# A hybrid attention layer: norm of the forgetting heads' output inside the attention stage, compression three couples later, and another order behind steps with extra work

## The chip, the cores and the metric

One core of one Trainium2 chip runs the whole layer in one launch. The metric is device time in microseconds (us), the median of several runs. The engines are TensorE (PE; PEld is its weight load), VectorE (DVE), ScalarE (ACT), GpSimd (POOL) and the DMA queue of SyncE (SP). Each runs its own instructions in order, and they meet at semaphores.

## The reference

The layer takes 512 prompt tokens and 8 sampled tokens (one each for 8 sequences with 256 cached positions), model width 1024, all in float32. Cut to what matters:

```python
hp  = half_ffn(x, ...)                               # x + 0.5 * rmsnorm(swiglu(rmsnorm(x)))
fq, fk, fv, logf, nq, nkv, ng = project(rmsnorm(hp), w_in, b_f, pos)
o_fox = fox_attention(fq, fk, fv, cumsum(logf), pos)     # 8 heads, forgetting bias, causal
o_nsa = nsa_attention(nq, ng, nkv, ...)                  # 8 heads: compressed + selected + window, gated
of = rmsnorm(o_fox.reshape(B, T, 512), g_fox)
on = rmsnorm(o_nsa.reshape(B, T, 512), g_nsa)
hp = hp + rmsnorm(concat([of, on]) @ w_out, g_mix_post)
y  = half_ffn(hp, ...)
# compress(x, w1, w2, pe): windows of 32 tokens, stride 16: gelu(hid) @ w2
```

The sampled tokens go through the same functions with the paged cache as keys and values. The two output norms (`of`, `on`) are separate, over 512 channels each.

## The kernel before

Activations lie transposed: 128 partitions of channels, 520 tokens along the free dimension. A weight item is 128 output channels; `products` multiplies it as a sum of three products of split halves (XH*WH, XL*WH, XH*WL), 8 channel tiles x 3 products x 2 token halves = 48 matmuls. ScalarE casts the high half of each item (L411), VectorE subtracts the low half (L414). The order is: first feed-forward, 23 items of the input projection, attention, 8 items of the output projection, second feed-forward.

**Attention** is 48 couples of (head, query tile) units, numbered m. Couples 0 to 15 are the forgetting heads, 16 to 47 the other heads' selected and window branches. The query tile is m mod 4, so scores are 128, 256, 384 and 512 columns wide in turn. The steps of the loop on TensorE are `scores(2m)` (L1559, the bias L1565, the mask L1567), the transposes of the weights of couple m-3 (`turn_p`, L1576), and the product with the values of couple m-4 (`weigh`, L1592). Scores of couple m need the exponentials of couple m-2, because four PSUM banks alternate. VectorE copies the even transposed unit out (L480), takes the maxima (`largest`, L1122), inverts the sums (L1128) and scales the weights of wide couples (L464); ScalarE copies the odd unit (L480), takes exponentials (L816) and copies finished output tiles to OT (`pair_out`, L800); GpSimd scales narrow couples (L464).

**Guests** are other work in PSUM banks 4 and 5 at fixed steps `AT_*`: first layer of the compression (AT_HIDDEN, step 11, L1622), its second layer (AT_CMP_KV, 15), compressed scores (AT_CMP_SCORES, 17, L1644), the decode's gate pick (AT_PICK, 18), its forgetting keys (AT_FOX_KEYS, 22, L1672), transposed compressed weights (AT_CMP_BACK, 25, L1652), the other decode keys (AT_NSA_KEYS, 26, L1681), transposed decode weights (AT_TURN, 30), decode values (AT_VALUES, 34, L1712) and the decode's output (AT_DECODED, 37). In a guest step TensorE first waits for the copies of the couple before (`banks_free`), runs the guest, `weigh(m-4)` and the scores of couple m+1, waits until the guest's banks are read (`emptied`), and only then does its `turn_p`. The functions `guest(m)` and `follow(m)` on the other engines hold the counterparts; on VectorE and ScalarE each step begins with the copy out (L480), then the maxima or exponentials.

SyncE loads what the guests need in one order: cache pages and shifted copies into X for the compression (L550 to L574), keys KF, KD and KW, values VS, then, after `cmp_back`, the forgetting values VF (L617), then VW (L621), and after `d_ot` (the decode's output) the output projection's weights.

**Behind attention**: ScalarE copies the last tile, both engines split the first two weight items, ScalarE squares 8 tiles of OT (L904), VectorE adds the squares (L1313), TensorE sums over partitions with a matrix of ones (L1441), ScalarE takes logarithm and exponential (L907, L910), VectorE multiplies (L1318), ScalarE and VectorE write the halves XH (L913) and XL (L944), while TensorE runs matmuls that nothing reads (L1448). Then 8 items are multiplied; VectorE copies each out of PSUM (L1327).

## Time and profile before

| | us |
|---|---|
| median of 3 runs | 1234.79 (1234.27 to 1239.14) |
| the profiled execution | 1235.9 |
| its span, first to last instruction | 1233.8 |
| PE busy | 1172.7 (95%) |
| DVE / ACT / POOL busy | 531.0 / 420.3 / 140.0 |
| mean granted TensorE clock | 0.977 of full speed |

Times in rows are counted from the start of the span. The granted clock is a share of 2.4 GHz, so 0.50 is the lower level of 1.2 GHz. Matmul ends are modelled, so starts are the safer numbers. An idle time stands in brackets with what ended it. Attention runs from 562 to 754 us, its end to the first product of the output projection from 754 to 770.

### The profile page before, as it was taken

How to read it: one execution, taken by the hardware profiler on the slowest of the kernel's cores; microseconds unless marked ns; L12 is line 12 of the kernel's file. 1: busy time of each engine (PE TensorE's matmuls, PEld its weight loads, DVE VectorE, ACT ScalarE, POOL GpSimd, SP SyncE). 2: the span in 40 equal slices, each digit the busy share in tenths (PEclk: the TensorE clock that was granted, in tenths of full speed). 3: DMA queues.
4: the chain of work that ended last, by engine and by line, in shares of the span. 5: the costliest groups of instructions: out<-in, count | busy, mean ns of one | idle time of the engine just before them, and what ended most of it. 6: DMA issues, size and time to landing. Idle time of an engine off the chain costs nothing.

```text
span 1233.8 us, 23263 instructions
## 1 busy us (share of the span) xinstructions
PE 1172.7 (95%) x9475; PEld 1078.7 (87%) x9482; DVE 531.0 (43%) x785; ACT 420.3 (34%) x731; POOL 140.0 (11%) x137
## 2 busy tenths in 40 slices
PE   8999999999999899998788997989999999999994
PEld 6999999999999799995354554979999999999994
DVE  3433433333333743454167676455343323333334
ACT  5322321222233642225144456444222221222332
POOL 0101100011111000222023110210011000011110
PEclk9999999999999999998889998999999999999997
DMA  7322223322223134216544311121222223232221
GB/s 273 103 71 99 86 78 110 104 74 96 78 86 112 54 121 139 85 61 157 119 121 120 121 69 35 69 69 43 95 102 78 70 101 112 85 103 87 67 86 70
DMA packets 49007, 117.52 MB, mean 95 GB/s; under 512 B 8186, under 2 KB 24954, under 8 KB 43138
## 3 DMA queue, kind: packets, MB, share of 16 engines
q1 hardware_dynamic: 45746, 110.55, 27.4%
q10 hardware_dynamic: 3184, 5.88, 1.3%
q8 instruction: 56, 0.92, 0.3%
q14 instruction: 21, 0.17, 0.0%
HBM read 107.79 MB, written 7.97 MB: 94 GB/s over the span
## 4 chain that ended last, share of the span: by engine, by line
PE 85%; DVE 6%; issue 3%; SPq 2%; ACT 2%; DMA 2%; DVEq 0%; ACTq 0%
PE ps L1432 75%; PE ps L1441 1%; PE ps L1622 1%; PE ps L1592 1%; PE ps L1559 1%; PE ps L1576 1%; DVE UT L964 1%; SPq L555 1%; DVE H L968 1%; DVE row_max L1122 1%; DVE PTS L480 1%; DVE XL L944 1%; DMA RAW<-in_w_gu 1%; DMA X<-X 1%; PE ps L1525 0%
## 5 line engine op out<-in xcount | busy, mean ns | idle before, releaser
L1432 PE MATMUL ps<-XH,WH 128*128 128x260 f32 x1904 | 389.8, 286 | 9.0 <-DVE XL L944 9.0
L1432 PE MATMUL ps<-XH,WL 128*128 128x260 f32 x1904 | 383.7, 283 | 0.0
L1432 PE MATMUL ps<-XL,WH 128*128 128x260 f32 x1904 | 383.2, 283 | 0.0
L411 ACT CAST WH<-RAW 128x1024 fp32r<-128x1024 f32 (+2 forms) x183 | 174.8, 956 | 528.1 <-PE ps L1432 525.9
L1432 PEld LDWEIGHTS ps<-XH,WH 128*128 128x128 f32 x1904 | 295.3, 189 | 14.9 <-DVE XL L944 10.3
L1432 PEld LDWEIGHTS ps<-XH,WL 128*128 128x128 f32 x1904 | 293.7, 189 | 0.0
L1432 PEld LDWEIGHTS ps<-XL,WH 128*128 128x128 f32 x1904 | 293.0, 188 | 0.0
L414 DVE TENSOR_TENSOR WL<-RAW,WH 128x1024 fp32r<-128x1024 f32 (+2 forms) x183 | 203.7, 1113 | 163.3 <-ACT WH L411 162.1
L1432 PE MATMUL ps<-UL,WH 128*128 128x260 f32 x704 | 141.9, 283 | 0.0
L1432 PE MATMUL ps<-UH,WL 128*128 128x260 f32 x704 | 141.5, 282 | 0.0
L1432 PE MATMUL ps<-UH,WH 128*128 128x260 f32 x704 | 141.3, 282 | 0.0
L1355 POOL TENSOR_TENSOR UL<-HT,UH 128x520 f32 (+1 forms) x44 | 57.8, 1315 | 634.8 <-ACT UH L692 634.8
L1432 PEld LDWEIGHTS ps<-UH,WL 128*128 128x128 f32 x704 | 108.5, 188 | 0.0
L1432 PEld LDWEIGHTS ps<-UH,WH 128*128 128x128 f32 x704 | 108.5, 188 | 0.0
L1432 PEld LDWEIGHTS ps<-UL,WH 128*128 128x128 f32 x704 | 108.4, 188 | 0.0
L984 DVE TENSOR_TENSOR UT<-ps,token_rstd 128x520 f32<-128x520 f32 x44 | 30.8, 700 | 145.8 <-PE ps L1432 145.8
L980 DVE TENSOR_TENSOR GT<-ps,token_rstd 128x520 f32<-128x520 f32 x44 | 30.8, 700 | 129.7 <-PE ps L1432 119.9
L692 ACT CAST UH<-HT 128x520 f32 (+1 forms) x44 | 27.6, 627 | 86.5 <-DVE HT L991 86.5
L1097 DVE TENSOR_TENSOR TR<-ps,token_rstd 128x520 f32<-128x520 f32 x23 | 16.1, 700 | 66.9 <-PE ps L1432 44.6
L1122 DVE TENSOR_REDUCE row_max<-ps 128x2 f32<-128x256 f32 (+3 forms) x48 | 39.1, 815 | 9.7 <-PE ps L1567 9.7
L816 ACT ACTIVATE PRB<-ps,row_max 128x384 f32<-128x384 f32 (+1 forms) x48 | 30.0, 630 | 25.6 <-DVE row_max L1122 24.5
L480 DVE COPY PTS<-ps 128x128 f32<-128x128 f32 (+3 forms) x48 | 23.5, 489 | 34.1 <-PE ps L1576 25.5
(239 smaller groups left out, 910.9 us busy)
## 6 DMA issues: line engine op xcount, KB each, us to landing
RAW<-in_w_gu SPq DMA_DIRECT2D x44, 1024.0 KB, 4.8
RAW<-in_w_down SPq DMA_DIRECT2D x16, 768.0 KB, 4.5
RAW<-in_w_in SPq DMA_DIRECT2D x11, 1024.0 KB, 5.0
RAW<-in_w_down SPq DMA_DIRECT2D x16, 640.0 KB, 4.3
KF<-in_fox_k SPq DMA_DIRECT2D x16, 256.0 KB, 4.2
VF<-in_fox_v SPq DMA_DIRECT2D x16, 256.0 KB, 5.0
RAW<-in_w_out SPq DMA_DIRECT2D x4, 1024.0 KB, 5.3
H<-in_x SPq DMA_DIRECT2D x4, 520.0 KB, 8.3
```

The lines of the kernel that those rows point to most:

```text
L411: nc.scalar.copy(WH[:, par, 0:width], RAW[:, slot, j, 0:width]).then_inc(w_hi, 1)
L414: nc.vector.tensor_tensor(WL[:, par, 0:width], RAW[:, slot, j, 0:width], WH[:, par, 0:width], ALU.subtract).then_inc(w_lo, 1)
L480: copy(PTS[:, w % PT_SLOTS, 0:i + 1, :], ps[:, 4 + w % 2, 0:P * (i + 1)].rearrange("p (a n) -> p a n", n=P)).then_inc(sem(name), 1)
L555: sp.dma_start(X[0:64, :, SEQ // PAGE + g, :, :].rearrange("p g n c -> p g (n c)"), I["nsa_t"][bass.ds(page[g], 1), :, 0:2, :].rearrange(" ...
L692: nc.scalar.copy(row(UH, st.m), HT[:, st.par, :]).then_inc(sem("hid_hi"), 1)
L816: nc.scalar.activation(weights(v)[:, 0:W], ps[:, score_bank(v), 0:W], ACT.Exp, bias=row_max[:, v:v + 1], accum_out=row_sum[:, v:v + 1]).th ...
L980: nc.vector.tensor_tensor(two(GT[:, st.par, :]), halves(0), two(R1[:, :]), ALU.mult).then_inc(sem("evac"), 1)
L984: nc.vector.tensor_tensor(two(UT[:, st.par, :]), halves(1), two(R1[:, :]), ALU.mult).then_inc(sem("evac"), 1)
L1097: nc.vector.tensor_tensor(two(TR[:, j % 4, :]), halves(j % 2), two(R1[:, :]), ALU.mult).then_inc(sem("projected"), 1)
L1122: nc.vector.reduce_max(row_max[:, v:v + 2], ps[:, score_bank(v):score_bank(v) + 2, 0:W], AX.X, negate=True).then_inc(sem("att_max"), 1)
L1355: nc.gpsimd.tensor_tensor(row(UL, st.m), HT[:, st.par, :], row(UH, st.m), ALU.subtract).then_inc(sem("hid_lo"), 1)
L1432: q = nc.tensor.matmul(ps[:, 2 * slot + half, 0:HALF], w[:, par, cols], x[:, kt0 + kt, half * HALF:(half + 1) * HALF], start=first and kt ...
```

## The change

1. The guest steps move: AT_HIDDEN 11 to 14, AT_CMP_KV 15 to 18, AT_CMP_SCORES 17 to 20, AT_CMP_BACK 25 to 27, AT_PICK 18 to 19, AT_NSA_KEYS 26 to 25, AT_TURN 30 to 29, AT_VALUES 34 to 32, AT_DECODED 37 to 35; AT_FOX_KEYS stays at 22. A guest AT_SUMS is added at 40.
2. In a step behind a guest VectorE takes the maxima and ScalarE the exponentials before the copy out.
3. The decode queries are filled in by 6 wider copies instead of 16, and the 8 copies of the new keys into KF go from VectorE to GpSimd, at step 17.
4. Eight of the sixteen loads of VF are issued ahead of the wait for `cmp_back`.
5. The forgetting heads' norm is computed in steps 36 to 48: squares on ScalarE, their sums on GpSimd, the partition sum on TensorE at 40, logarithm and exponential on ScalarE, the multiplication on GpSimd, XH on ScalarE and XL on VectorE. The first two weight items are split in steps 41 to 43. OSQ moves to another region.
6. Behind attention only tiles 4 to 7 are left. TensorE multiplies the ready tiles 0 to 3 of items 0 and 1 around the second partition sum; the matmuls that nothing reads are gone there.

```diff
-AT_HIDDEN, AT_CMP_KV, AT_CMP_SCORES, AT_CMP_BACK = 11, 15, 17, 25
-AT_PICK, AT_FOX_KEYS, AT_NSA_KEYS, AT_TURN, AT_VALUES, AT_DECODED = 18, 22, 26, 30, 34, 37
+AT_HIDDEN, AT_CMP_KV, AT_CMP_SCORES, AT_CMP_BACK = 14, 18, 20, 27
+AT_PICK, AT_FOX_KEYS, AT_NSA_KEYS, AT_TURN, AT_VALUES, AT_DECODED, AT_SUMS = 19, 22, 25, 29, 32, 35, 40
...
-            sp.wait_ge(sem("cmp_back"), 2)
-            for g in range(NPAGE):
+            for g in (*range(8, NPAGE), *range(8)):
+                if g == 0:
+                    sp.wait_ge(sem("cmp_back"), 2)
                 sp.dma_start(VF[g // 8][:, g % 8, :],
@@ ScalarE @@
+                elif m == AT_SUMS:
+                    output_log(0)
...
+                elif m == AT_DECODED + 1:
+                    act.wait_ge(sem("o_all"), 1)
+                    act.wait_ge(sem("att_out"), 5)
+                    output_square(0)
+                    output_square(1)
+                elif m == AT_DECODED + 2:
+                    output_square(2)
+                    output_square(3)
+                elif m == AT_DECODED + 3:
+                    output_square(4)
+                elif m == AT_SUMS:
+                    output_rstd(0)
+                    act.wait_ge(sem("att_out"), 6)
+                    act.wait_ge(sem("oacc"), 3)
+                    output_square(5)
+                elif m in (AT_SUMS + 1, AT_SUMS + 2):
+                    split(IT_OUT + m - AT_SUMS - 1)
+                elif AT_SUMS + 4 <= m < AT_SUMS + 8:
+                    output_high(m - AT_SUMS - 4)
+                elif m == AT_SUMS + 8:
+                    act.wait_ge(sem("att_out"), 7)
+                    output_square(6)
...
+                    if m < PAIRS and m - 1 in GUESTS:
+                        exponentials(m)
                     if m >= 3 and m not in GUESTS:
                         turn_out(act, nc.scalar.copy, 2 * (m - 3) + 1, "att_odd_out")
-                    if m < PAIRS:
+                    if m < PAIRS and m - 1 not in GUESTS:
                         exponentials(m)
...
+            output_square(7)
+            output_log(1)
+            output_rstd(1)
+            for t in range(4, 8):
+                output_high(t)
@@ VectorE @@
-                    for h in range(HF):
-                        nc.vector.tensor_copy(view(QBF[part, h // 2, :], h, [[128, 2], [40, 4]]), ...)
-                        q = nc.vector.tensor_copy(view(QBN[kv, :], h, [[128, 2], [40, 4]]), ...)
+                    for odd in (0, 1):
+                        part = slice(64 * odd, 64 * odd + 64)
+                        nc.vector.tensor_copy(view(QBF[part, :, :], odd, [[DEC * 32 + 2, 4], [128, 2], [40, 4]]), ...)
+                        for kv in range(HKV):
+                            q = nc.vector.tensor_copy(
+                                view(QBN[64 * kv:64 * kv + 64, :], 4 * kv + odd, [[2, 2], [128, 2], [40, 4]]), ...)
                     q.then_inc(sem("qb_filled"), 1)
-                    for n in range(DEC):
-                        q = nc.vector.tensor_copy(KF[n][:, :, PAST], fk_new[:, :, KF_ORDER[n]])
-                    q.then_inc(sem("kf_new"), 1)
...
+                if m in (AT_SUMS + 2, AT_SUMS + 3):
+                    split(IT_OUT + m - AT_SUMS - 2)
+                if AT_SUMS + 5 <= m < AT_SUMS + 9:
+                    low("o", "out", m - AT_SUMS - 5)
...
+                    if m < PAIRS and m - 1 in GUESTS:
+                        largest(m)
                     if m >= 3 and m not in GUESTS:
                         turn_out(dve, nc.vector.tensor_copy, 2 * (m - 3), "att_even_out")
-                    if m < PAIRS:
+                    if m < PAIRS and m - 1 not in GUESTS:
                         largest(m)
@@ GpSimd @@
+                if m == AT_PICK - 2:
+                    pool.wait_ge(sem("att_scored"), 4 * HF)
+                    nc.gpsimd.memset(QBF[:, :, :], 0.0).then_inc(sem("qb_cleared"), 1)
+                    pool.wait_ge(sem("cmp_hid"), 2)
+                    for n in range(DEC):
+                        q = nc.gpsimd.tensor_copy(KF[n][:, :, PAST], fk_new[:, :, KF_ORDER[n]])
+                    q.then_inc(sem("kf_new"), 1)
...
-                elif m == AT_CMP_SCORES + 8:
+                elif m == AT_FOX_KEYS + 1:
...
+                elif m == AT_DECODED + 2:
+                    output_sum(1)
+                    output_sum(2)
+                    output_sum(3)
+                elif m == AT_SUMS:
+                    output_sum(5)
+                elif AT_SUMS + 1 <= m < AT_SUMS + 5:
+                    t = m - AT_SUMS - 1
+                    pool.wait_ge(sem("orstd"), 1)
+                    nc.gpsimd.tensor_tensor(OT[:, t, :], OT[:, t, :], OR[:, 0, :], ALU.mult).then_inc(
+                        sem("onormed"), 1)
...
             attention()
+            output_sum(6)
@@ TensorE @@
+                elif m == AT_SUMS:
+                    pe.wait_ge(sem("oacc"), 3)
+                    all_partitions(OACC[:, 0, :], 2).then_inc(sem("oss"), 1)
...
+                elif m == AT_SUMS:
+                    pe.wait_ge(sem("oss_ln"), 1)
...
-            for g in (0, 1):
-                pe.wait_ge(sem("oacc"), 3 * g + 3)
-                all_partitions(OACC[:, g, :], 2 + g).then_inc(sem("oss"), 1)
-            keep_warm(WARM[2], bank=0)
+            def operand(t, kt):
+                if t == 0:
+                    pe.wait_ge(sem("xlo"), since("xlo", "o", kt + 1))
+                cols = slice(kt * P, kt * P + P)
+                for p, (w, x) in enumerate(((WH, XH), (WH, XL), (WL, XH))):
+                    for half in (0, 1):
+                        q = nc.tensor.matmul(ps[:, 2 * t + half, 0:HALF], w[:, (IT_OUT + t) % 2, cols], ...)
+                return q
...
+            ready(IT_OUT)
+            operand(0, 0)
+            operand(0, 1)
+            pe.wait_ge(sem("oacc"), 5)
+            all_partitions(OACC[:, 1, :], 2, stop=False)
+            pe.wait_ge(sem("osq"), 8)
+            all_partitions(OSQ[:, 2, :], 2, start=False).then_inc(sem("oss"), 1)
+            operand(0, 2)
+            operand(0, 3)
+            ready(IT_OUT + 1)
+            for kt in range(4):
+                operand(1, kt)
+            for t, kt in ((0, 4), (0, 5), (1, 4), (0, 6)):
+                operand(t, kt)
+            operand(0, 7).then_inc(used, 1)
+            operand(1, 5)
+            operand(1, 6)
+            operand(1, 7).then_inc(used, 1)
+            for t in range(2, KT):
```

## Rows read from the trace of the kernel before

**Rows 1.** Windows by stage: engines' busy time, granted clock, DMA share, GB/s.
```profile
722.00:754.00 32.00, 29.99 (x278) 19.07 (x275) 21.11 (x47) 17.83 (x55) 5.06 (x10) 1.00 0.16 64
754.00:769.90 15.90, 9.03 (x28) 4.72 (x29) 10.70 (x15) 11.67 (x19) 0.00 (x0) 0.68 0.21 66
```

**Rows 2.** Timeline of TensorE around the first layer of the compression.
```profile
580.25 0.39 PE L1576 MATMUL ps<-consts,PRA 128*128 128x128 f32 x2
...
587.13 1.04 PE L1576 MATMUL ps<-consts,PRB 128*128 128x128 f32 x8
...
597.20 18.38 PE L1622 MATMUL ps<-X,W 128*128 128x336 f32 x32 [6.51 <-DMA X<-X]
```

**Rows 3.** Timeline of TensorE in step 21.
```profile
656.11 0.85 PE L1576 MATMUL ps<-consts,PRB 128*128 128x128 f32 x6 [2.08 <-DVE PTS L480]
```

**Rows 4.** Timeline of VectorE in step 19: 16 copies like the first, then KF.
```profile
652.54 0.16 DVE L1237 COPY QBN<-nq_new 64x8 f32<-64x8 f32 x1
...
654.97 0.67 DVE L1241 COPY KF<-fk_new 128x4 f32<-128x4 f32 x8
```

**Rows 5.** Windows (columns as in group 1): the clock behind the compressed scores and behind step 21.
```profile
638.00:647.00 9.00, 8.38 (x50) 5.44 (x48) 3.99 (x7) 1.71 (x5) 2.09 (x3) 0.50 0.00 0
656.50:661.00 4.50, 4.15 (x35) 1.77 (x36) 4.43 (x9) 2.25 (x9) 0.61 (x2) 0.63 0.65 170
```

**Rows 6.** Timeline of TensorE: the same product at either clock.
```profile
638.43 1.12 PE L1592 MATMUL ps<-PTS,VTF 128*64 128x128 f32 x8
...
656.89 0.66 PE L1592 MATMUL ps<-PTS,VTN 128*64 128x128 f32 x8
```

**Rows 7.** Timeline of TensorE: waits of and behind guests.
```profile
671.55 1.06 PE L1652 MATMUL ps<-consts,SCM 128*128 128x128 f32 x8
...
674.74 0.87 PE L1576 MATMUL ps<-consts,PRB 128*128 128x128 f32 x6 [0.47 <-ACT PCT L841]
...
676.29 1.93 PE L1681 MATMUL ps<-KD,QBN 128*32 128x257 f32 x16 [0.68 <-ACT PTS L480]
...
718.85 0.70 PE L1559 MATMUL ps<-KXN,QXN 64*128 64x256 f32 x4 [1.07 <-ACT PRB L816]
```

**Rows 8.** Timeline of ScalarE: the idle time ahead of a wide couple's exponentials.
```profile
736.81 0.69 ACT L816 ACTIVATE PRB<-ps,row_max 128x512 f32<-128x512 f32 x1 [1.08 <-DVE row_max L1122]
```

**Rows 9.** Timeline of ScalarE behind attention.
```profile
754.07 0.59 ACT L800 COPY OT<-ps 128x512 f32<-128x512 f32 x1 [2.39 <-PE ps L1599]
...
756.45 0.64 ACT L904 ACTIVATE OACC<-OT 128x520 f32<-128x520 f32 x1
...
764.89 0.69 ACT L907 ACTIVATE OR<-ps,consts 128x520 f32<-128x520 f32 x1 [1.05 <-PE ps L1441]
765.61 0.64 ACT L910 ACTIVATE OR<-OR 128x520 f32<-128x520 f32 x1
...
774.79 0.73 ACT L913 ACTIVATE XH<-OT,gains 128x520 fp32r<-128x520 f32 x1 [0.55 <-DVE OT L1318]
```

**Rows 10.** Timeline of VectorE behind attention.
```profile
774.07 0.69 DVE L1318 TENSOR_TENSOR OT<-OT,OR 128x520 f32<-128x520 f32 x1
774.68 0.75 DVE L944 SCALAR_TENSOR_TENSOR XL<-OT,gains,XH 128x520 fp32r<-128x520 f32 x1
...
778.61 1.23 DVE L414 TENSOR_TENSOR WL<-RAW,WH 128x1024 fp32r<-128x1024 f32 x1 [0.45 <-ACT WH L411]
783.18 0.70 DVE L1327 COPY Y<-ps 128x520 f32<-128x520 f32 x1 [3.34 <-PE ps L1432]
```

**Rows 11.** The chain of waits: one item, and a partition sum at full clock.
```profile
507.02 5.72 PE ps L1432 x48
...
835.92 0.88 PE ps L1441 x4
```

**Rows 12.** GpSimd: 18 additions of squares, and one beside VectorE's subtraction.
```profile
L1348 POOL TENSOR_TENSOR ACC<-ACC,SQ x18: 1303/1315/1886, 358.3 to 1210.4; 128x520 f32<-128x520 f32 x18
...
784.85 1.87 POOL L1348 TENSOR_TENSOR ACC<-ACC,SQ 128x520 f32<-128x520 f32 x1 [4.54 <-ACT SQ L640]
```

More of the change, by code:

```diff
@@ L67 @@
 GUESTS = (AT_HIDDEN, AT_CMP_KV, AT_CMP_SCORES, AT_CMP_BACK, AT_PICK, AT_FOX_KEYS, AT_NSA_KEYS, AT_TURN, AT_VALUES,
-          AT_DECODED)
+          AT_DECODED, AT_SUMS)
 TILES = (["fg"] + ["fq"] * 4 + ["fk"] * 4 + ["fv"] * 4
@@ L822, in decode_exp, with output_square, output_log, output_rstd @@
                                      accum_out=dsum[:, n:n + 1]).then_inc(sem("d_exp"), 1)
+            def output_square(t):
+                dst = OACC[:, t // 4, :] if t % 4 == 0 else OSQ[:, t % 4 - 1, :]
+                nc.scalar.activation(dst, OT[:, t, :], ACT.Square).then_inc(sem("osq"), 1)
+            def output_log(g):
+                act.wait_ge(sem("oss"), g + 1)
+                nc.scalar.activation(two(OR[:, g, :]), halves(2), ACT.Ln, scale=1.0 / 512,
+                                     bias=const("eps")[:, 0:1]).then_inc(sem("oss_ln"), 1)
+            def output_rstd(g):
+                act.wait_ge(sem("oss_ln"), g + 1)
+                nc.scalar.activation(OR[:, g, :], OR[:, g, :], ACT.Exp, scale=-0.5).then_inc(sem("orstd"), 1)
+            def output_high(t):
+                act.wait_ge(sem("onormed"), t + 1)
+                nc.scalar.activation(XH[:, t, :], OT[:, t, :], ACT.Copy, scale=gain("out", t)).then_inc(
+                    sem("xhi"), 1)
             def guest(m):
@@ L1280, in follow @@
                                             ALU.mult).then_inc(sem("d_pn"), 1)
-                elif m == AT_VALUES:
+                if m == AT_VALUES:
                     nc.vector.reduce_sum(OS[:, 0, :], view(EF[:, :, :, :], 0, [[1, DH], [DH, 2 * HF]]), AX.X)
@@ L1818, in _ @@
             attention()
-            for g in (0, 1):
-                pe.wait_ge(sem("oacc"), 3 * g + 3)
-                all_partitions(OACC[:, g, :], 2 + g).then_inc(sem("oss"), 1)
-            keep_warm(WARM[2], bank=0)
-            for t in range(KT):
+            def operand(t, kt):
[4 more added lines that the diff above has]
+                    for half in (0, 1):
+                        q = nc.tensor.matmul(ps[:, 2 * t + half, 0:HALF], w[:, (IT_OUT + t) % 2, cols],
+                                             x[:, kt, half * HALF:(half + 1) * HALF],
+                                             start=kt == 0 and p == 0, stop=kt == KT - 1 and p == 2)
+                return q
[18 more added lines that the diff above has]
+            for t in range(2, KT):
                 ready(IT_OUT + t)
```

85 lines of the change are left out of this document (30 added, 55 removed).

## The prediction

> **What bounds the kernel now.** I read the page first: TensorE is busy for 1172.7 of 1233.8 us, so time is won where it stands idle or runs at 1.2 GHz. The windows by stage say where the change touches such time: between 722 and 754 us TensorE works 29.99 of 32 us at granted clock 1.00, and between 754 and 770 only 9.03 of 15.9 at 0.68, of which most is matmuls that nothing reads [rows 1]. The timeline of TensorE then shows single waits: 6.51 us for the shifted copies of X at step 11 [rows 2], 2.08 us for VectorE's copy out [rows 3], and waits of 0.4 to 1.1 us around guests [rows 7]. In the windows the reader is to see the clock: 0.50 for 9 us behind the 64 tiny matmuls of the compressed scores, and 0.63 behind the wait of rows 3 [rows 5]. What one such us costs is in rows 6: the same eight matmuls take 1.12 us at 0.50 and 0.66 at 1.00.
>
> **The change part by part.**
>
> *Compression at step 14.* Ahead of the guest there now stand the transposes and products of steps 11 to 13 and the scores of 12 to 14. The same pieces one cycle of four couples earlier run from 580.25 to the transposes at 587.13: 6.9 us [rows 2]. TensorE was free from about 590.7 (597.20 less 6.51), so it comes to the guest at 597.6, and the copies of X, which depend on nothing that moved, release it at 597.2. The work fills the wait: -6.5. If the copies came later, the difference would be waited for, so the gain lies between 0 (copies 6.5 late) and 6.5; they are queued behind nothing new, so I take -6.5.
>
> *Queries and keys of the decode.* In step 19 VectorE made 16 copies and eight into KF, from 652.5 to 655.6, 3.1 us, ahead of a copy out that TensorE stood still for, 2.08 us [rows 3, 4]. Now 6 copies remain, some 1.1 us by the spacing in rows 4, and the KF copies are on GpSimd three steps early. They stand in step 20 behind the 1.2 us maximum of the compressed scores, ahead of the maxima of 21 and the copy out that the forgetting keys at 22 wait for (`banks_free`), so some wait returns there: I take 0.5. With it goes the dip to 0.63 over 4.5 us, in which TensorE was busy for 4.15 [rows 5]: 0.37 of that is 1.5, but much of it is in small matmuls that such a dip need not stretch, so I take -0.6, and part of the waits next to it, -0.5. Sum -2.1 - 0.6 - 0.5 + 0.5 = -2.7; bounds -4 and 0. The 9 us at 0.50 behind the compressed scores stay: the 64 matmuls are unchanged and now have the tiny pick next to them. GpSimd's eight tiny copies have no row; between 0.1 us (VectorE's, rows 4) and 1.3 us (a full one, rows 12) each they take 1 to 10 us. They run in steps 17 to 19; steps 18 and 19 are scaled by VectorE, so even the long end only delays the scaling of couple 20, needed at 23. I cost it at nothing.
>
> *Maxima and exponentials first.* Behind a guest the scores are ready before the transposes. The 1.07 us behind AT_VALUES is of that kind [rows 7]; there are eleven guests, so I take that and half as much again for the others. Against it, the copy out comes up to 1.2 us later. -1.5; bounds -3 and +1.
>
> *AT_CMP_BACK at 27.* `weigh(23)` in that same step needs both copies of the transposed weights. Before, the guest came two steps ahead, and `emptied` cost 0.47 [rows 7]. Now ScalarE's copy of 0.6 us stands behind the exponentials of a wide couple: from the end of its scores 1.2 (maxima) + 1.35 + 0.6 = 3.3 us with the hand-overs, while TensorE has 1.06 (guest) and 1.09 (`weigh`). Wait 1.2 to 1.4, less 0.47: +0.9; bounds 0 and 1.5. Of the SyncE queue: eight VF loads go earlier; eight and VW still follow `cmp_back`, with about 15 us until AT_VALUES at 32. I cost that at nothing.
>
> *AT_SUMS.* One partition sum, 0.88 us [rows 11], and one more `banks_free`, 0.68 as in rows 7, taken as 0.5: +1.4. The wait for `oss_ln` lies beside `weigh(36)` and the scores of 41, 1.3 us, against 0.7 of the logarithm.
>
> *Work on the other engines, steps 36 to 48.* ScalarE gets 7 squares, a logarithm, an exponential, four XH at 0.64 to 0.73 us and two splits at 1.05: 4.5 + 1.3 + 2.9 + 2.1 = 10.8 us [rows 9]; it has 32 - 17.8 = 14.2 free [rows 1]. VectorE gets 2 x 1.23 + 4 x 0.75 = 5.5 [rows 10], with 10.9 free. Before a wide couple's exponentials ScalarE is idle for 1.08 us [rows 8], which hides a square or an XH. What shows: VectorE's split in step 43, whose idle time is smaller, +0.5, and the last couple, where nothing runs ahead: `low` twice (1.5 us, partly in its waits) ahead of the last copies out, +1.3. Sum +1.8; bounds 0 and, if all of ScalarE's work is on the path, +10.8.
>
> *Behind attention.* Let E be the end of the last product, 754.0 [rows 9]. Before, item 2 starts when item 1 is done, at 783.18 [rows 10], E + 29.2. Now: copy 0.6 and square 0.64, E + 1.2. TensorE meanwhile does tiles 0 and 1 of item 0, 12 of an item's 48 matmuls, 1.44 us [rows 11]. The two partition sums take 1.8: E + 3.2. Logarithm and exponential 1.4, multiplication 0.69, XH 0.73, XL 0.75 [rows 9, 10]: XL of tile 4 at E + 6.9, tile 5, 6 and 7 at 1.3 us intervals (VectorE's 0.69 + 0.75, overlapped by 0.1), the last at E + 10.8. TensorE's six ready pieces of 0.72 fill E + 3.2 to E + 7.5; tiles 4, 5, 4, 6 run to E + 10.4; tile 7 ends at E + 11.6, and the last three of item 1 at E + 13.8. Item 2's WL comes 2.4 us after item 0 (783.18 less 5.7 to 778.61 + 1.23), E + 14.0; I take E + 14.1. 29.2 - 14.1 = 15.1: -15.1. Below that TensorE can't go by more than its waits, 13.3 us of work, -15.9; if the clock fell to 0.68 as before [rows 1], the 13.3 us would take 6.3 more.
>
> Sum: -6.5 - 2.7 - 1.5 + 0.9 + 1.4 + 1.8 - 15.1 = -21.7. From the profiled execution's 1235.9 that is 1214.2. The median shown is 1234.8, 1.1 lower, so 1213.1.
>
> **A rule weighed.** GpSimd's additions of squares take 1.315 us alone and 1.87 where they start inside VectorE's two-input subtraction [rows 12]: one of the two waits. The Trainium skill, SBUF — State Buffer, "Who interferes with whom", says that the two engines share one pair of ports, that the instruction that starts first holds it for its whole length, and that VectorE's two-input operations and its two-port `tensor_scalar` both need it. By that rule, the trace agrees for GpSimd as the one who waits; the other order is no row here.
>
> **The rivals.**
> 1. *ScalarE or VectorE bounds steps 36 to 48.* For it: 10.8 us into 14.2 free, in an order of instructions that leaves no choice; ScalarE's free time comes in pieces of 0.4 to 1.1 us. Against it: TensorE is the one that is full (94%). If most of ScalarE's work is on the path, 8.5 instead of 1.8: 1220.
> 2. *GpSimd holds up VectorE.* Four sums and four multiplications of 1.3 us run beside VectorE's scaling. If each delays one scaling by half its length and half of that is hidden, 8 x 0.65 / 2 = 2.6: 1215.7. This is the rule above as a mechanism.
> 3. *The clock falls behind attention.* The last step's waits are longer than before and the sums come early; at 0.68 the gain there is 8.8 instead of 15.1: 1219.4.
> 4. *Slower: the attention stage stays at 1.2 GHz.* Guests 18, 19 and 20 now stand together, with tiny matmuls in each, at the place where the clock was 0.50 for 9 us [rows 5]. A step of some 2.4 us takes 1.7 times as long there [rows 6], 1.7 us more. If 15 more steps ran so, +25: 1238. It decides from 13 such steps on. Against it: before, the clock came back in four steps.
> 5. *The moved guests don't do what they say*, because X or VF comes later than TensorE: the 6.5 and the 2.7 go, 1222.
>
> **Chances.** Forecast 0.58, rival 1 0.18, rival 2 0.10, rival 3 0.06, rival 4 0.03, rival 5 0.05. The range starts at 1205, with every bound of the middle terms low (-1.3, -1.5, -0.9, -1.8 and some waits that I have not seen), and ends at 1222, with rivals 1, 2, 3 and 5 in it. A change of 0.5%, 6.2 us, is about what a measurement of this kernel can tell. Only rival 4 is outside on the other side: faster 0.95, same 0.02, slower 0.03.
>
> **What would show it.** Right: in the profile after, the first layer of the compression starts at 597 to 598 with a wait under 0.5 us; no wait for the copy out of 2 us behind it; the window from the last product of attention to item 2 is 14 us at clock 1.00; a wait of 1 to 1.5 us in step 27. Wrong: steps 36 to 48 longer than 34 us with waits for ScalarE's exponentials (rival 1); GpSimd's additions or VectorE's scalings longer than alone (rival 2); a clock under 0.9 behind attention (rival 3); a stretch of 0.50 longer than 12 us (rival 4). A time above 1222 would mean that a wait at the decode's guests that I cost at nothing is there.

## The result, and the profile after

| | before | after |
|---|---|---|
| median | 1234.68 (1233.69 to 1239.14, 7 runs) | 1228.88 (1225.81 to 1230.65, 7 runs) |
| the profiled execution | 1235.9 | 1230.65 |
| its span | 1233.8 | 1228.8 |
| DVE / ACT / POOL busy | 531.0 / 420.3 / 140.0 | 528.4 / 419.2 / 153.8 |

The ratio of after to before is 0.995, interval 0.9935 to 0.9965: 5.8 us faster, where 21.7 were forecast and 1205 was the low end and 1222 the high end of the range. The time lies 6.9 us above that range.

A stretch is told here from the start of `scores(m)` (the first matmul of couple m's scores) to that of another, since these exist in every kernel. "Lead" is how much earlier after reaches a point than before.

| us from the span's start | before | after | lead |
|---|---|---|---|
| scores of 28 | 686.26 | 682.21 | 4.1 |
| scores of 36 | 716.26 | 714.42 | 1.8 |
| scores of 40 | 727.08 | 724.26 | 2.8 |
| scores of 47 | 743.74 | 750.33 | -6.6 |
| last product of attention ends | 753.97 | 763.98 | -10.0 |
| item 2 starts | 783.2 | 778.01 | 5.2 |

So attention ends 10.0 us later instead of 6.6 earlier (21.7 less 15.1), and the stretch behind it does what was forecast: 29.2 us before, 14.0 now. The windows of after (columns as in rows 1) show the two stages of [rows 1] again:

```profile
722.00:754.00 32.00, 26.64 (x206) 15.86 (x204) 24.43 (x43) 20.38 (x58) 17.05 (x18) 0.89 0.11 34
764.00:778.00 14.00, 13.53 (x104) 12.88 (x104) 7.41 (x11) 7.81 (x12) 0.82 (x1) 1.00 0.00 1
```

The reader is to see the fifth engine: GpSimd's busy time in the same 32 us went from 5.06 to 17.05, TensorE's went from 29.99 to 26.64 and the granted clock from 1.00 to 0.89. Behind attention TensorE is busy 13.53 of 14 us at 1.00.

**GpSimd's queue.** ScalarE's last two squares, then GpSimd's timeline in after, steps 37 to 47:

```profile
720.28 1.16 ACT L827 ACTIVATE OSQ<-OT 128x520 f32<-128x520 f32 x2
```

```profile
722.33 1.09 POOL L464 TENSOR_SCALAR PRA<-PRA,row_inv,gates 128x256 f32<-128x256 f32 x2 [1.95 <-DVE row_inv L1159]
723.38 4.14 POOL L1445 TENSOR_TENSOR OACC<-OACC,OSQ 128x520 f32<-128x520 f32 x3
...
737.12 1.98 POOL L464 TENSOR_SCALAR PRA<-PRA,row_inv,gates 128x256 f32<-128x256 f32 x2 [1.28 <-DVE row_inv L1159]
739.07 4.00 POOL L1436 TENSOR_TENSOR OT<-OT,OR 128x520 f32<-128x520 f32 x3
...
756.23 1.28 POOL L1445 TENSOR_TENSOR OACC<-OACC,OSQ 128x520 f32<-128x520 f32 x1 [3.79 <-ACT OSQ L827]
```

The squares are all there at 721.4, but the three additions stand in the queue behind the scaling of a narrow couple that is ready only at 722.3, and run together from 723.4. VectorE beside them (timeline of VectorE, its scalings L464 and the subtractions L414 and L975):

```profile
724.76 2.97 DVE L464 TENSOR_SCALAR PRB<-PRB,row_inv,gates 128x384 f32<-128x384 f32 x2
...
736.94 1.20 DVE L414 TENSOR_TENSOR WL<-RAW,WH 128x1024 fp32r<-128x1024 f32 x1
739.58 2.35 DVE L464 TENSOR_SCALAR PRB<-PRB,row_inv,gates 128x384 f32<-128x384 f32 x2
741.86 2.30 DVE L414 TENSOR_TENSOR WL<-RAW,WH 128x1024 fp32r<-128x1024 f32 x1
...
753.36 0.87 DVE L464 TENSOR_SCALAR PRB<-PRB,row_inv,gates 128x384 f32<-128x384 f32 x2
...
756.26 1.81 DVE L975 SCALAR_TENSOR_TENSOR XL<-OT,gains,XH 128x520 fp32r<-128x520 f32 x1
```

The same pair of scalings takes 0.87 at 753.36, with GpSimd idle, and 2.97 and 2.35 where an addition or a multiplication of GpSimd is under way; the weight's subtraction 1.20 and 2.30; XL 0.75 [rows 10] and 1.81. TensorE is what waits for these (its timeline, steps 40 to 48):

```profile
727.66 1.99 PE L1492 MATMUL ps<-OACC,consts 128*128 128x260 f32 x4 [2.69 <-POOL OACC L1445]
...
744.63 1.36 PE L1627 MATMUL ps<-consts,PRB 128*128 128x128 f32 x6 [2.15 <-DVE PTS L480]
755.38 0.90 PE L1627 MATMUL ps<-consts,PRB 128*128 128x128 f32 x6 [1.50 <-DVE PTS L480]
758.68 1.94 PE L1627 MATMUL ps<-consts,PRB 128*128 128x128 f32 x8 [1.82 <-DVE PTS L480]
```

These are four waits, 8.2 us in all, and behind the first, the second and the last the clock falls. Windows of after:

```profile
728.00:730.00 2.00, 2.00 (x8) 1.02 (x7) 1.14 (x4) 1.11 (x5) 0.00 (x0) 0.50 0.00 0
744.00:748.00 4.00, 3.37 (x18) 2.22 (x18) 3.69 (x10) 3.15 (x12) 0.83 (x1) 0.60 0.68 202
758.00:764.00 6.00, 5.32 (x40) 4.37 (x41) 1.23 (x3) 0.58 (x1) 0.00 (x0) 0.72 0.00 0
```

The partition sum shows it in one row: 1.99 us at 0.50, against 0.88 at full clock [rows 11].

**The guests.** TensorE's waits of after at them, to be held against [rows 2, 3, 7]:

```profile
596.96 18.28 PE L1673 MATMUL ps<-X,W 128*128 128x336 f32 x32 [2.05 <-DMA X<-X]
...
629.41 0.87 PE L1682 MATMUL ps<-HID,W 128*128 128x160 f32 x2 [2.37 <-DVE HID L1250]
...
666.43 1.93 PE L1732 MATMUL ps<-KD,QBN 128*32 128x257 f32 x8 [2.27 <-DVE KW L1287]
...
681.15 1.12 PE L1650 MATMUL ps<-PCT,VCZ 128*128 128x512 f32 x2 [1.05 <-ACT PCT L860]
```

The 2.08 us of [rows 3] is gone and the 6.51 of [rows 2] became 2.05. The wait at the compression's second layer (2.37) was 1.80 in before, and a new one of 2.27 stands at the other decode keys, which moved from step 26 to 25. VectorE's timeline ahead of it:

```profile
661.84 1.21 DVE L1273 TENSOR_REDUCE csum<-SCM 128x32 f32<-128x1024 f32 x1
663.08 0.35 DVE L1274 RECIPROCAL csum<-csum 128x32 f32<-128x32 f32 x1
...
664.44 1.00 DVE L464 TENSOR_SCALAR PRB<-PRB,row_inv,gates 128x512 f32<-128x512 f32 x2
665.36 0.15 DVE L1281 RECIPROCAL dinv<-dsum 64x1 f32<-64x1 f32 x1
665.54 0.35 DVE L1282 TENSOR_SCALAR SF<-SF,dinv 64x257 f32<-64x257 f32 x1
665.92 0.17 DVE L1285 COPY KD<-nk_new 128x8 f32<-128x8 f32 x1
666.01 0.17 DVE L1287 COPY KW<-nk_new 128x8 f32<-128x8 f32 x1
```

VectorE works without a gap, and two copies of 0.17 us that depend on none of it stand last. The clock falls here too, in the window behind the wait:

```profile
666.00:670.00 4.00, 3.57 (x31) 1.90 (x32) 0.83 (x4) 1.02 (x4) 2.99 (x4) 0.57 0.00 0
```

### The profile page after: what moved, and what is told of

The parts are those of the page before. It is cut to its first block, busy times and chain, and to the rows that moved or that the text cites. A ratio compares the mean times of both kernels' runs of the same rounds, so it can differ in the third digit from the quotient of the medians.

```text
span 1228.8 us, 23220 instructions
## 1 busy us (share of the span) xinstructions
PE 1169.5 (95%) x9460; PEld 1080.0 (88%) x9466; DVE 528.4 (43%) x757; ACT 419.2 (34%) x731; POOL 153.8 (13%) x154
## 4 chain that ended last, share of the span: by engine, by line
PE 86%; DVE 6%; issue 2%; SPq 2%; ACT 2%; DMA 1%; POOL 0%; DVEq 0%; ACTq 0%; POOLq 0%
PE ps L1483 75%; PE ps L1492 2%; PE ps L1673 1%; PE ps L1643 1%; PE ps L1610 1%; PE ps L1627 1%; DVE UT L995 1%; SPq L555 1%; DVE H L999 1%; DVE row_max L1153 1%; DVE PTS L480 1%; DMA X<-X 1%; PE ps L1884 1%; DVE XL L975 1%; PE ps L1576 0%
## 5 line engine op out<-in xcount | busy, mean ns | idle before, releaser
L1483 PE MATMUL ps<-XH,WH 128*128 128x260 f32 x1872 | 383.4, 286 | 8.4 <-DVE XL L975 8.0
L1483 PE MATMUL ps<-XH,WL 128*128 128x260 f32 x1872 | 377.6, 283 | 0.0
L1483 PE MATMUL ps<-XL,WH 128*128 128x260 f32 x1872 | 377.0, 283 | 0.0
L1483 PEld LDWEIGHTS ps<-XH,WH 128*128 128x128 f32 x1872 | 290.7, 189 | 13.1 <-DVE XL L975 8.3
L1483 PEld LDWEIGHTS ps<-XH,WL 128*128 128x128 f32 x1872 | 289.0, 189 | 0.0
L1483 PEld LDWEIGHTS ps<-XL,WH 128*128 128x128 f32 x1872 | 288.3, 189 | 0.0
L414 DVE TENSOR_TENSOR WL<-RAW,WH 128x1024 fp32r<-128x1024 f32 (+2 forms) x183 | 204.8, 1119 | 158.1 <-ACT WH L411 156.8
L1483 PEld LDWEIGHTS ps<-UL,WH 128*128 128x128 f32 x704 | 108.3, 188 | 0.0
L1373 POOL TENSOR_TENSOR ACC<-ACC,SQ 128x520 f32<-128x520 f32 x18 | 27.0, 1499 | 93.1 <-ACT SQ L641 93.1
```

Of the source, the lines that this page charges most:

```text
L414: nc.vector.tensor_tensor(WL[:, par, 0:width], RAW[:, slot, j, 0:width], WH[:, par, 0:width], ALU.subtract).then_inc(w_lo, 1)
L1373: nc.gpsimd.tensor_tensor(ACC[:, :], ACC[:, :], SQ[:, par, :], ALU.add).then_inc(sem("acc"), 1)
L1483: q = nc.tensor.matmul(ps[:, 2 * slot + half, 0:HALF], w[:, par, cols], x[:, kt0 + kt, half * HALF:(half + 1) * HALF], start=first and kt ...
```

## The experiments

Twelve kernels ran in three groups, each group beside runs of the kernel before. Single executions of one kernel spread over 1 to 9 us (before: 1229.4 to 1238.6 in 23 runs), so differences of under 2 us between two experiments are read from stretches of the trace and not from medians.

| kernel | median | ratio to before, 95% | scores of 40 to end of attention |
|---|---|---|---|
| after | 1228.88 | 0.9950, 0.9935 to 0.9965 | 39.7 |
| norm off | 1230.75 | 0.9982, 0.9964 to 1.0000 | 26.9 |
| order back | 1227.91 | 0.9960, 0.9943 to 0.9978 | 40.7 |
| sums on TensorE | 1227.45 | 0.9965, 0.9943 to 0.9987 | 36.3 |
| fills for the norm | 1223.70 | 0.9929, 0.9905 to 0.9953 | 33.0 |
| guests back | 1233.53 | 1.0009, 0.9990 to 1.0027 | 26.9 |
| late guests back | 1229.91 | 0.9970, 0.9955 to 0.9985 | 26.9 |
| keys on GpSimd | 1227.93 | 0.9951, 0.9934 to 0.9969 | 26.9 |
| multiplications on VectorE | 1223.85 | 0.9926, 0.9900 to 0.9952 | 35.3 |
| reductions later | 1226.85 | 0.9942, 0.9924 to 0.9960 | 26.9 |
| lows late | 1221.72 | 0.9899, 0.9882 to 0.9915 | 31.8 |
| all edits | 1217.80 | 0.9873, 0.9856 to 0.9889 | 31.8 |
| all edits, old order | 1216.09 | 0.9853, 0.9830 to 0.9876 | 31.8 |

Before has 26.9 in the last column. The medians of before were 1233.6 (norm off to fills), 1233.0 (guests back to multiplications) and 1233.7 (the last four).

**Norm off.** Parts 5 and 6 of the change undone, parts 1 to 4 kept.

```diff
-                elif m == AT_DECODED + 2:
-                    output_sum(1)
...
-                elif AT_SUMS + 1 <= m < AT_SUMS + 5:
...
+            for g in (0, 1):
+                pe.wait_ge(sem("oacc"), 3 * g + 3)
```

> The changed kernel without parts 5 and 6 (the norm is computed behind attention as before, all other parts kept). The table of score starts shows the changed kernel 1.5 to 2.8 us ahead at steps 36 to 40 and 10.0 us behind at the end of attention. Theory A (the norm's own work in steps 36 to 48 is what costs the 12.8 us): the 15.1 us behind attention are lost again and about 12.8 are won back, 1228.9 + 2.3 = 1231, and the last product of attention ends 2 to 4 us earlier than in the kernel before, at 750 to 752. Rival B (the moved guests and the new order upset the late steps as well): attention ends at 755 or later and the time is 1236 or more.

Its trace takes 26.9 us from the scores of 40 to the end, as before, and its lead of 3.1 us stays constant there. So all 12.8 us that attention lost behind step 40 come from parts 5 and 6, and at the end of attention the guests, copies and order together give 3.1 of the 9.8 forecast.

**Order back.** Part 2 alone undone, on VectorE and ScalarE.

```diff
-                    if m < PAIRS and m - 1 in GUESTS:
-                        exponentials(m)
                     if m >= 3 and m not in GUESTS:
                         turn_out(act, nc.scalar.copy, 2 * (m - 3) + 1, "att_odd_out")
-                    if m < PAIRS and m - 1 not in GUESTS:
+                    if m < PAIRS:
                         exponentials(m)
```

> The changed kernel with maxima and exponentials behind the copy out again in all steps (part 2 undone). My forecast's view: part 2 gives 1.5 us, so this is 1.5 us slower, 1230.4. Rival: the copies out that now come up to 1.2 us later cost as much as the earlier exponentials bring; then this is the same within 1 us or up to 3 us faster.

The scores of 15 to those of 40 take 107.3 us instead of 108.3, and 40 to the end 40.7 instead of 39.7. The time is the same, as the rival said. The forecast -1.5 for this part is not there. Single steps do change: from the scores of 22 to those of 23 it takes 5.5 instead of 6.7 us (after has a wait of 1.15 at the forgetting keys, this kernel none) and from 34 to 35 3.3 instead of 4.5, so in these two the new order costs 1.1 to 1.2; from 25 to 26 it is 10.0 instead of 9.2, so there it brings 0.8.

**Sums on TensorE.** The three additions of squares of GpSimd are left out, and TensorE sums four squares over partitions into one bank instead of one.

```diff
-                    pe.wait_ge(sem("oacc"), 3)
-                    all_partitions(OACC[:, 0, :], 2).then_inc(sem("oss"), 1)
+                    pe.wait_ge(sem("osq"), 4)
+                    for t in range(4):
+                        q = all_partitions(OSQ[:, t - 1, :] if t else OACC[:, 0, :], 2, start=t == 0, stop=t == 3)
+                    q.then_inc(sem("oss"), 1)
```

> The changed kernel, but the forgetting heads' squares are summed on TensorE (4 pairs of partition-sum matmuls instead of 1) and GpSimd's three additions at step 37 are gone. Theory A1 (TensorE waits 2.69 us for those additions, which stand behind the scaling of couple 37, and VectorE's scaling beside them takes 2.97 instead of 0.87 us, and the clock falls to 0.50 behind the wait): 2.7 + 1.1 + about 1 go, 2.6 us of matmuls are added, -2 us, and VectorE's scaling is back at 0.87. Rival (the wait only moves to the exponentials or to the copies out): the same time or up to 2 us slower.

The stretch from the scores of 40 to the end is 3.4 us shorter although TensorE has twelve matmuls more. The wait of 2.69 is gone and the scaling of 2.97 is 0.87 again; the multiplications are still there, and so are a scaling of 2.36, a subtraction of 2.30 and the wait of 2.15 behind them. The medians don't resolve the 3.4: the two ratios overlap, and this kernel and after were not timed side by side.

**Fills for the norm.** GpSimd's additions and multiplications are each replaced by eight fills of 65 columns, which read nothing; the norm's values are left out of the result.

```diff
-                    nc.gpsimd.tensor_tensor(OT[:, t, :], OT[:, t, :], OR[:, 0, :], ALU.mult).then_inc(
-                        sem("onormed"), 1)
+                    only_write(OT[:, t, :]).then_inc(sem("onormed"), 1)
```

> The changed kernel, but every addition and multiplication that the early norm puts on GpSimd is replaced by eight fills of 65 columns of the same destination, which read nothing (the norm's values are left out so). Theory P (GpSimd holds a port that VectorE needs, as the scalings of 2.97 and 2.35 us and the split of 2.30 us beside GpSimd's instructions suggest): these return to 0.87 and 1.23 us even though GpSimd is as busy, the 2.15 us wait at step 46 goes and so do half-speed stretches: -3 to -6 us. Rival (VectorE's instructions are long for another reason, and GpSimd's place in the queue is what costs): they stay long, and the time changes only by what shorter fills save, under 1.5 us.

Attention behind step 40 is 6.7 us shorter than in after. VectorE's timeline in this kernel:

```profile
726.31 0.87 DVE L464 TENSOR_SCALAR PRB<-PRB,row_inv,gates 128x384 f32<-128x384 f32 x2
...
738.15 2.23 DVE L464 TENSOR_SCALAR PRB<-PRB,row_inv,gates 128x384 f32<-128x384 f32 x2
740.30 1.22 DVE L414 TENSOR_TENSOR WL<-RAW,WH 128x1024 fp32r<-128x1024 f32 x1
...
752.04 0.75 DVE L975 SCALAR_TENSOR_TENSOR XL<-OT,gains,XH 128x520 fp32r<-128x520 f32 x1
```

and GpSimd's:

```profile
724.90 2.77 POOL L1441 MEMSET OACC<- 128x65 f32 x24
...
737.62 2.16 POOL L1441 MEMSET OT<- 128x65 f32 x24
...
751.99 0.81 POOL L1441 MEMSET OACC<- 128x65 f32 x8 [3.74 <-ACT OSQ L827]
```

XL is the two-input instruction that runs beside fills here: 0.75, as alone, against 1.81 beside an addition in after. The subtraction at 740.30 starts when the fills are over, so its 1.22 says nothing of fills. The scaling behaves in two ways: at 738.15 it stands still until the fills end (2.23), at 726.31 it takes 0.87 in the midst of fills. The Trainium skill, SBUF — State Buffer, "Who interferes with whom", says that a GpSimd instruction that only writes does not hold up a VectorE instruction with two inputs, but contends with a `tensor_scalar` in its two-port mode, where whoever starts first keeps the other waiting. The trace agrees for the two inputs at XL, and for the scaling at 738.15 but not visibly at 726.31.

The 6.7 us are not all due to the missing reads: 24 fills take 2.16 or 2.77 us where three additions took 4.14 and three multiplications 4.00. The wait for the sum fell from 2.69 to 1.31 and the one of 2.15 to 0.94. How the 6.7 divide between shorter instructions and missing reads stays open.

**Guests back.** Norm off, and the guests at their steps of before; order and copies stay.

```diff
-AT_HIDDEN, AT_CMP_KV, AT_CMP_SCORES, AT_CMP_BACK = 14, 18, 20, 27
+AT_HIDDEN, AT_CMP_KV, AT_CMP_SCORES, AT_CMP_BACK = 11, 15, 17, 25
-AT_PICK, AT_FOX_KEYS, AT_NSA_KEYS, AT_TURN, AT_VALUES, AT_DECODED = 19, 22, 25, 29, 32, 35
+AT_PICK, AT_FOX_KEYS, AT_NSA_KEYS, AT_TURN, AT_VALUES, AT_DECODED = 18, 22, 26, 30, 34, 37
```

> The kernel without the early norm, and with every guest at its step of before; the order behind guests, the wider copies, the keys on GpSimd and the early half of the VF loads stay. Attention ends at 753.97 in the kernel before and at 750.86 with the moved guests (norm_off). Forecast's view (the moved guests bring 5.6 us net, order and copies 4.2): attention ends at 749.8 plus what the clock gives, and norm_off should have been at 744. Theory C (the moved guests win the 6.5 us wait and lose most of it again at steps 24 to 35, where the later compression and the earlier decode guests meet): this ends within 1.5 us of norm_off, at 750 to 752. Rival D (order and copies brought nothing, the moved guests the 3.1 us): it ends at 753 to 755.

The time is that of before (1.0009). The wait for X is 8.31 us here, more than the 6.51 of before, since this run came to the guest 2.8 us earlier and X releases it at 596.2 (before 597.2, after 597.0). Attention ends at 752.4, 1.5 before before's and 1.6 behind norm off's: 0.1 beyond theory C's bound, and short of rival D's 753 to 755. Moving the guests is thus worth 1.6 us in the traces (750.9 against 752.4) and 3.3 by the ratios, and order and copies 0 to 1.5.

That small sum hides two larger differences, between kernels with their guests at the same steps. The scores of 15 to those of 24 take 39.9 us where before took 44.4, at a clock of 0.91 against 0.85, without the wait of 2.08. The scores of 36 to those of 40 take 14.4 us where before took 10.8. ScalarE's timeline in before, then in this kernel:

```profile
714.29 0.27 ACT L480 COPY PTS<-ps 128x128 f32<-128x128 f32 x1 [0.48 <-PE ps L1576]
```

```profile
712.05 0.69 ACT L817 ACTIVATE PRB<-ps,row_max 128x512 f32<-128x512 f32 x1 [3.35 <-DVE row_max L1143]
...
713.39 0.26 ACT L480 COPY PTS<-ps 128x128 f32<-128x128 f32 x1
```

TensorE's timeline in this kernel, and a window:

```profile
713.79 0.61 PE L1601 MATMUL ps<-consts,PRA 128*128 128x128 f32 x2 [1.02 <-ACT PTS L480]
```

```profile
714.00:718.00 4.00, 4.00 (x24) 2.00 (x23) 2.35 (x8) 2.28 (x9) 0.59 (x2) 0.50 0.06 10
```

In the new order ScalarE's copy out stands behind the exponentials of a wide couple, and these wait for maxima that stand behind VectorE's two reductions (1.92 and 0.57 us, from 708.46). The copy comes 2.2 us behind the start of the scores of 36 instead of 2.0 ahead of it. TensorE waits about as long in all (1.75 us, before 1.48) but for the copies, early in the stretch, and the clock over it is 0.76 where before has 1.00. So the order costs something at the old guest steps too, and the 3.5 us are mostly the clock.

**Late guests back.** Norm off, and only the four late guests at their old steps (AT_NSA_KEYS 26, AT_TURN 30, AT_VALUES 34, AT_DECODED 37).

> The kernel without the early norm; only the decode guests behind step 22 go back (decode keys 26, transposes 30, values 34, output 37), the compression stays three couples late. Between steps 24 and 36 norm_off loses 6.2 us of its lead (8.3 to 2.2). Theory C1 (that loss is because the decode keys at 25 wait 2.3 us for VectorE's copies of new keys, queued behind the compression's sums, and because the values at 32 come ahead of narrow couples, whose maxima wait for 2.5 us of reductions): 2 to 4 us of it come back, attention ends at 747 to 749. Rival (what is lost comes from the compressed weights at 27 and from the number of guests, not from where the decode's stand): it ends at 750.5 to 752.

From the scores of 24 to the end it takes 90.5 us and norm off 90.2, the rival's result. But the sum hides two differences of 4 us. From the scores of 24 to those of 36 this kernel takes 49.3 us and norm off 53.4: the theory's 2 to 4 us do come back, with a wait of 0.90 at the other decode keys. From 36 to 40 it takes 14.3 and norm off 9.9, in the same way as guests back (a wait of 1.03 for ScalarE's copy out, a clock of 0.76). So it does matter where these guests stand. This run was 3.6 us ahead already at step 24, on the same code (see the last section).

**Keys on GpSimd.** Norm off, and the two copies of the new keys into KD and KW go from VectorE to GpSimd, a step earlier.

```diff
-                    dve.wait_ge(sem("kd_in"), 16 * NPAGE)
-                    nc.vector.tensor_copy(KD[:, :, PAST], nk_new[:, 0, :])
...
+                    pool.wait_ge(sem("kd_in"), 16 * NPAGE)
+                    nc.gpsimd.tensor_copy(KD[:, :, PAST], nk_new[:, 0, :])
```

> The kernel without the early norm, with the two copies of the decode's new keys on GpSimd in step 23 instead of VectorE in step 24. Theory C1 (TensorE stands 2.3 us at the decode keys for them, and its clock falls to 0.50 behind it, where the first product takes 3.5 instead of 1.9 us): the step from the scores of 25 to those of 26 shortens from 9.2 to 5.5 us and attention ends 2 to 4 us earlier, 747 to 749. Rival (VectorE's maxima of couple 25 and the copy out are as late, so TensorE waits for those at the same place): the step stays above 7.5 us, the end within 1 us of 750.9.

TensorE's timeline at the guest:

```profile
664.34 1.93 PE L1705 MATMUL ps<-KD,QBN 128*32 128x257 f32 x16
```

No wait is left, and the clock stays at 1.00 between 666 and 670. The scores of 25 to those of 26 take 5.3 us instead of 9.2; of these 3.9, 2.3 are the wait and the rest is the clock. At the end of attention 2.9 of them are left (measured from the scores of 24); from the scores of 28 to those of 32 it takes 14.0 us and norm off 12.9, with the clock at 0.50 from 684.0 to 687.4 here and at 1.00 there.

**Multiplications on VectorE.** Sums on TensorE, and the four multiplications of the norm go to VectorE.

> The changed kernel with the forgetting heads' squares summed on TensorE and their four multiplications on VectorE in steps 41 to 44 instead of on GpSimd. From the scores of 40 to the end of attention the changed kernel takes 39.7 us, the one with sums on TensorE 36.3, the one whose GpSimd instructions read nothing 33.0. Theory P (shared port: a multiplication of 1.3 us on GpSimd costs VectorE more than doing it itself in 0.69 us): 32 to 34.5 us, total about 1224 to 1226. Rival L (VectorE is full in these steps, so 2.8 us more on it are 2.8 us more on the path): 36.5 to 39 us.

The stretch takes 35.3 instead of 36.3 us: VectorE has 2.8 us more to do and is still done earlier, though above the 32 to 34.5 that theory P expected. The scaling is 0.87 and the subtraction 1.22 again, the wait of 2.15 is 0.75. What is left are 1.23 and 1.82 in the last two couples. TensorE's timeline and window:

```profile
746.60 0.90 PE L1623 MATMUL ps<-consts,PRB 128*128 128x128 f32 x6 [1.23 <-DVE PTS L480]
...
749.91 1.07 PE L1623 MATMUL ps<-consts,PRB 128*128 128x128 f32 x8 [1.82 <-DVE PTS L480]
```

```profile
752.00:756.00 4.00, 4.00 (x32) 3.19 (x29) 0.00 (x0) 0.59 (x2) 0.00 (x0) 0.72 0.00 0
```

**Reductions later.** Keys on GpSimd, and the two reductions of the decode's output (1.92 and 0.57 us on VectorE in after) move from step 32's follow-up to that of 33.

```diff
-                if m == AT_VALUES:
+                if m == AT_VALUES + 1:
                     nc.vector.reduce_sum(OS[:, 0, :], ...)
```

> The kernel with the norm off GpSimd and the two new-key copies on GpSimd, and the decode output reductions moved from step 31 to behind the maxima of step 33. Theory (VectorE's queue at step 31 is the wait): the stretch from the scores of couple 32 to those of 36, 18.2 us in the kernel it starts from (692.50 to 710.7), becomes 1 to 2 us shorter, the 1.0 us wait for PTS at the read after the scores of 35 is gone, the time 1226.5. Rival (the reductions only move the wait): the same stretch stays within 0.5 us, the time 1228.

The stretch from the scores of 32 to those of 36 is 17.6 us; in the kernel that it starts from it is 19.3 (692.50 to 711.76; the 18.2 in the expectation is wrong). That is 1.7 shorter, and the wait of 1.02 for PTS is gone: the theory is right.

**Lows late.** Sums and multiplications as above, and XL of tiles 2 and 3 and XH of tile 3 stand behind the last copies out.

```diff
-                if AT_SUMS + 5 <= m < AT_SUMS + 9:
+                if AT_SUMS + 5 <= m < AT_SUMS + 7:
...
+            low("o", "out", 2)
+            low("o", "out", 3)
             for t in range(4, 9):
```

> The kernel with the sums of squares on TensorE and the multiplications of the norm on VectorE, and the low halves XL of tiles 2 and 3 and the high half XH of tile 3 moved behind the last copies out. Theory (the splits of item 2's input hold VectorE ahead of the last weights): from the scores of 40 to the end of attention 35.3 us becomes 33.5, the tail from there to item 2 stays 14 to 15 us, the time 1222.3. Rival (what is taken from the couples is paid behind them): attention ends 1.5 to 2 us earlier, the tail grows by as much, the time stays 1223.9.

The stretch is 31.8, 3.5 less, twice the 1.8 expected. TensorE's timeline and a window:

```profile
750.75 0.95 PE L1627 MATMUL ps<-consts,PRB 128*128 128x128 f32 x6 [0.57 <-DVE PTS L480]
...
752.63 1.06 PE L1627 MATMUL ps<-consts,PRB 128*128 128x128 f32 x8 [0.34 <-DVE PTS L480]
```

```profile
752.00:756.00 4.00, 3.66 (x43) 2.72 (x40) 2.51 (x5) 1.44 (x3) 1.16 (x1) 1.00 0.00 0
```

The waits fell by 2.1; the other 1.4 is the clock, which no longer falls to 0.72 behind them. The tail is 14.0 (756.61 to 770.64), as in after. The rival is false: the tail does not grow by what is moved into it.

**All edits, and all edits with the old order.** The first has all the edits above; the second also undoes part 2.

> The four single edits together: three additions of squares as four sums on TensorE, four multiplications of the norm on VectorE, the two new-key copies on GpSimd, the reductions of the decode output at step 33, the low halves behind the last copies out. If the gains add (they lie in stretches that do not overlap): 1223.9 less 2.8 for the copies, 1.0 for the reductions and 1.5 for the low halves, 1218.6, range 1216 to 1221. Rival (what is gained ahead of step 40 is taken back by work that waits for transfers or by the clock): no better than 1222.

> As the kernel with all edits together, and the order maxima and exponentials first undone (the extra work stands ahead of them again). Theory (the order brings nothing once the extra work is on idle engines): within 1 us of it, 1218. Rival (the order did help where VectorE is full): 2 to 4 us slower, 1221 to 1223.

1217.8 and 1216.1: the gains add up, and both beat the kernel before by 1.3 and 1.5% and after by some 10 and 12 us. The intervals of the two overlap. In the traces the old order takes 101.4 us from the scores of 15 to those of 40 and the new one 104.8, but part of that is the clock (0.79 and 0.57 in the same 8 us, 628 to 636), and the pair after and order back gives 1.0 for the same edit. The step of the scores of 22 repeats in this pair (5.5 us in the old order, 6.8 in the new), while that of 34 is 2.8 in both once the reductions are out of the way. What is shown is that the new order brings nothing; that it costs 1 to 2 us is likely and not settled.

## Why the prediction was wrong

The profiled execution was forecast at 1214.2 and took 1230.65. The 16.5 us are 9.6 in the two terms of steps 36 to 48 and 7.0 in those of the guests, copies and order; the term of the tail is right to 0.1.

1. **Behind attention, -15.1: right.** Item 2 starts 14.03 us behind the last product (forecast 14.1) at clock 1.00. In all eight kernels with this tail, whatever ran before it, it is 14.02 to 14.05. Rival 3 did not come.

2. **"Work on the other engines, steps 36 to 48", +1.8, and AT_SUMS, +1.4: the step that failed.** Together 12.8 (39.7 less 26.9) instead of 3.2. The prediction added up busy time of ScalarE and VectorE against their free time, and had no term at all for GpSimd's eight instructions; as rival 2 it gave them 2.6 us with a chance of 0.10. The mechanism of rival 2 is right as to who is held up (taking GpSimd's instructions away brought scaling and subtraction back to 0.87 and 1.22 in multiplications on VectorE), and its price was wrong in three ways. First, each instruction was taken to delay one scaling by half its length; the delayed ones are 2.1, 1.5, 1.1 and 1.1 us longer than alone. Second, GpSimd's queue itself was not followed: its additions stand behind a scaling that waits until 722.3, so TensorE waited 2.69 for the sum, where I had looked only at `oss_ln` behind it. Third, the waits were priced without what follows them: 0.50 in 728 to 730, 0.60 in 744 to 748 and 0.72 in 758 to 764. By the runs, the sums on GpSimd cost 3.4 net of TensorE's twelve additional matmuls and the multiplications a further 1.1 net of VectorE's own; XL and XH in the last couples, priced at +1.3, cost 3.5, of which 1.4 is the clock. The 4.9 that remain over 26.9 are the four partition sums (1.10 and 2.79), a wait of 0.75 and small ones. These are differences of one profile each.

3. **Compression at 14, -6.5: right in its mechanism.** X released the guest at 596.96 (forecast 597.2). The wait that I forecast as under 0.5 was 2.05, since this run came 2.67 us earlier to it: the clock from 562 to 570 was 0.57 in before and 1.00 in after. From the start to the scores of 15 after gained 8.6 us.

4. **Copies of the decode, -2.7: the wait went, the time did not.** The 2.08 us is gone and no wait stands there. But the stretch that it lies in, from the scores of 15 to those of 24, takes 45.0 us in after and 44.4 in before, both at a clock of 0.85: TensorE has a wait of 1.03 there for ScalarE's copy out behind the compression, 2.37 instead of 1.80 at its second layer and 1.15 at the forgetting keys, and its waits are 7.2 us in all against 7.5. The prediction had 0.5 for all that returns.

   The guest steps added a second loss. The copies into KD and KW are as tiny as those into KF and stand at the end of a full VectorE queue too, and moving AT_NSA_KEYS a step forward put TensorE right behind them: 2.27 us and a dip of the clock, together 3.9, about 2.9 net (keys on GpSimd). The prediction's last sentence names such a wait; its sum has no term for it.

5. **Maxima and exponentials first, -1.5: wrong.** Order back is no slower. The wait behind AT_VALUES that the term rested on [rows 7] was for the reductions, which delay the maxima in either order; with them a step later the stretch is 1.7 shorter (reductions later). The new order only moved the wait to the copies out (guests back).

6. **AT_CMP_BACK at 27, +0.9: right.** The wait was forecast at 1.2 to 1.4 and is 1.05.

The forecast for these parts was -9.8; 2.8 came. After gains 8.6 us up to the scores of 15 and then loses against before: 0.6 from 15 to 24, 4.0 from 24 to 28, 1.0 from 28 to 32 and 0.3 from 32 to 40. The 4.0 are the decode keys, since with keys on GpSimd the stretch from 24 to 28 is 17.3, as in before. The loss in the first of these stretches, where a gain was forecast, is told by the waits under 4, and how much of it is the order is not settled. Rival 5 is false for X; rival 1 is right in part, as the last couples show; rival 4 did not come, the longest stretch with a clock of 0.57 or less in after is the 8 us from 642 to 650.

## What to carry to other kernels

When work is given to an idle engine, price it by its neighbours: which instructions of the other engines are held up while it runs, and which of its own queue stand ahead of it. Here parts 5 and 6 cost attention 12.8 us for the 15.2 that they saved behind it, and giving a piece of it to the busiest engine (four sums on TensorE instead of three additions on GpSimd) was cheaper. Price a wait of TensorE of about 2 us with the clock behind it: twice, taking away 2.1 to 2.3 us of waits took away 1.4 to 1.6 more (keys on GpSimd, lows late). And compare two kernels stretch by stretch: late guests back and norm off agree within 0.3 us from the scores of 24 to the end, with two opposite differences of 4 us inside.
